# Two transformer blocks on one core: the input issued first on the weights' queue, constants and angles moved into the first down-projection

## The reference, cut to what matters

```python
ang = positions.astype(jnp.float32)[..., None] * inv_freq      # used by the mixer's rope
lower_bounds = jnp.cumsum(jax.nn.softmax(hg_lb_logits, axis=0), axis=0)
h = h + 0.5 * swiglu(rms_norm(h, ln_ffn1[i]), w1_gate[i], w1_up[i], w1_down[i])   # "first SwiGLU"
u = rms_norm(h, ln_mix[i]) @ w_in[i]
...                                                            # hgrn2 + latent attention
h = h + jnp.concatenate([o_hg, o_mla], axis=-1) @ w_out[i]
h = h + 0.5 * swiglu(rms_norm(h, ln_ffn2[i]), w2_gate[i], w2_up[i], w2_down[i])   # "second SwiGLU"
...                                                            # gate, then the second block

def swiglu(x, w_gate, w_up, w_down):
    return (jax.nn.silu(x @ w_gate) * (x @ w_up)) @ w_down
def rms_norm(x, g):
    y = x * lax.rsqrt(jnp.mean(x * x, axis=-1, keepdims=True) + EPS)
    return y * g
```

## Time and profile before

| | us |
|---|---|
| median of 3 runs | 1607.98 (1607.02 to 1611.02) |
| the profiled execution | 1612.58 |
| its span, first to last instruction | 1610.8 |

### The profile page before, as it was taken

One profiled execution on the slowest core, in us unless ns is written; L12 is line 12 of the kernel. 1 busy time (PEld: TensorE's weight loads), 2 busy tenths in 40 slices (PEclk: granted clock), 3 DMA queues, 4 the chain that ended last, 5 costly groups with the idle time before them and its releaser, 6 DMA issues.

```text
span 1610.8 us, 21164 instructions
## 1 busy us (share of the span) xinstructions
PE 1404.9 (87%) x8066; PEld 1074.1 (67%) x8066; DVE 997.7 (62%) x1792; ACT 571.0 (35%) x955; POOL 709.2 (44%) x443
## 2 busy tenths in 40 slices
PE   8799899998999999998999998777777877777776
PEld 8799899978999998888889893333333332333332
DVE  3868434446688544561563577777777777777654
ACT  4554335423444344553443542222222222222212
POOL 2334336421334444386665485444444444444440
PEclk9899899999999999999999999999989999989999
DMA  8677453311576653244323379999999999999994
GB/s 334 216 253 258 159 183 132 131 53 64 180 279 241 248 184 126 68 155 157 104 80 119 107 277 423 421 422 421 422 421 422 421 422 421 422 422 422 421 422 176
DMA packets 59350, 427.15 MB, mean 265 GB/s; under 512 B 6592, under 2 KB 6912, under 8 KB 7936
## 3 DMA queue, kind: packets, MB, share of 16 engines
q0 software_dynamic: 36864, 268.45, 40.2%
q1 hardware_dynamic: 20736, 149.69, 26.4%
q10 hardware_dynamic: 1664, 7.86, 1.2%
HBM read 424.93 MB, written 1.05 MB: 264 GB/s over the span
## 4 chain that ended last, share of the span: by engine, by line
PE 34%; DMA 28%; issue 14%; DVE 13%; POOL 7%; ACT 4%; DVEq 0%; POOLq 0%; SPq 0%; ACTq 0%
DMA rows_x<-in_expert_uv,arena 26%; POOL wlo L326 6%; PE ps L861 4%; PE ps L421 4%; PE ps L864 4%; PE ps L426 4%; PE ps L422 4%; PE ps L498 2%; PE ps L499 2%; PE ps L500 2%; DMA ring<-in_w 2%; DVE arena L1675 1%; ACT whi L937 1%; DVE arena L1347 1%; DVE arena L1491 1%
## 5 line engine op out<-in xcount | busy, mean ns | idle before, releaser
L326 POOL TENSOR_TENSOR wlo<-ring,whi 128x1024 fp32r<-128x1024 f32 x162 | 406.9, 2521 | 512.8 <-ACT whi L937 512.3
L421 PE MATMUL ps<-nh,whi 128*128 128x256 f32 x1440 | 368.1, 292 | 21.6 <-DVE wlo L326 14.1
L937 ACT ACTIVATE whi<-ring 128x1024 fp32r<-128x1024 f32 x236 | 243.5, 1054 | 329.2 <-PE ps L426 130.3
L422 PE MATMUL ps<-nh,wlo 128*128 128x256 f32 x1440 | 358.7, 285 | 0.0
L421 PEld LDWEIGHTS ps<-nh,whi 128*128 128x128 f32 x1440 | 278.3, 193 | 28.6 <-DVE wlo L326 15.1
L422 PEld LDWEIGHTS ps<-nh,wlo 128*128 128x128 f32 x1440 | 278.9, 194 | 0.3
L426 PE MATMUL ps<-nl,whi 128*128 128x256 f32 x1440 | 210.6, 286 | 0.1
L326 DVE TENSOR_TENSOR wlo<-ring,whi 128x1024 fp32r<-128x1024 f32 x74 | 101.3, 1380 | 166.3 <-ACT whi L937 162.3
L426 PEld LDWEIGHTS ps<-nl,whi 128*128 128x128 f32 x1440 | 189.3, 193 | 5.4 <-DVE nl L1288 2.1
L1823 POOL DMA_INDIRECT arena<-in_expert_uv,arena x96 | 112.0, 1166 | 141.2 <-PE ps L864 129.6
L1675 DVE CUSTOM_DVE_ANT_0 arena<-arena 128x1024 f32<-128x1024 f32 x96 | 124.7, 1299 | 39.3 <-DMA arena<-in_expert_uv,arena 35.0
(11 more groups left out here) (324 smaller groups left out, 2426.4 us busy)
## 6 DMA issues: line engine op xcount, KB each, us to landing
ring<-in_w SPq DMA_DIRECT2D x118, 1024.0 KB, 4.9
arena<-in_wmod SPq DMA_DIRECT2D x24, 1024.0 KB, 5.0
small<-in_small ACTq DMA_DIRECT2D x1, 2816.0 KB, 10.8
arena<-in_expert_uv,arena POOLq DMA_INDIRECT x96, 26.8
h<-in_x ACTq DMA_DIRECT2D x1, 1024.0 KB, 7.8
keys<-in_keys ACTq DMA_DIRECT2D x1, 1024.0 KB, 20.8
rows_w<-in_expert_uv,arena POOLq DMA_INDIRECT x64, 25.6
lev_mask<-in_lev_mask ACTq DMA_DIRECT2D x1, 512.0 KB, 11.5
```

What stands on the lines that cost most here:

```text
L326: return v.tensor_tensor(wlo[:, tile % TILES, :], ring[:, tile // 2 % RAW, at:at + TILE], whi[:, tile % TILES, :].bitcast(F32), ALU.subtract)
L421: mm(to, hi[:, k, :], nh[:, k, :], start=(k == 0), stop=False)
L422: mm(to, lo[:, k, :], nh[:, k, :], start=False, stop=False)
L937: fn(whi[:, tile % TILES, :], ring[:, slot % RAW, at:at + TILE], ACT.Copy).then_inc(S("high_w"), 1)
```

## The change

**Input.** SP issues `x` in two halves of four of its eight blocks, ahead of the first two slots of the ring. ACT's squares wait for the half they read. ACT issues only `vec`, `con` and the positions. PE runs 36 matmuls on ones before the squares' sums in place of 26. PE's wait for `con` moves from behind the first SwiGLU to in front of the 12 matmuls on ones.

**Order at the start.** ACT takes the root before it makes the high parts of tiles 0 and 1. DVE takes the reciprocal first, then makes `wlo` of tile 0, then scales.

**Bulk constants.** `load_rest` is gone from ACT. SP issues the same bytes behind seven of the down slots' loads (`load_later`), `small` in three parts.

**Angles and bounds.** They leave the written-out pairs and go behind the residual updates 4, 5 and 6 of the down-projection on DVE; the exponential and the sines go behind squares 4 and 5 on ACT.

```diff
+            def load_later(i):
+
+                if i in (0, 2, 4):
+                    at = slice(i * N_SMALL // 6, (i + 2) * N_SMALL // 6)
+                    sp.dma_start(small[:, at], a["small"][:, at]).then_inc(S("small_landed"), 16)
+                if i == 1:
+                    sp.dma_start(lev_mask[:, :, :], a["lev_mask"]).then_inc(S("small_landed"), 16)
...
+                if i == 6:
+                    sp.dma_start(keys[:, :, :], a["keys"]).then_inc(S("small_landed"), 16)
...
                 for j in range(ahead + 1, slot + 2 * FB + DOWN_SLOTS + RAW):
                     load(j)
-
+                    if mod == 0:
+                        load_later(j - ahead - 4)
+
+            for half in range(2):
+                at = slice(half * C // 2, (half + 1) * C // 2)
+                sp.dma_start(h[:, at, :], a["x"][:, at, :]).then_inc(S(f"x_landed{half}"), 16)
             load(0)
             load(1)
...
             pe.wait_ge(S("constants"), 2)
-            keep_busy(26, bank=5)
+            keep_busy(36, bank=5)
             for c in range(C):
                 square_sum(0, c)
+            pe.wait_ge(S("con_landed"), 16)
             keep_busy(12, bank=5)
 
             swiglu(S_FFN1, 0, 0, 1, 0)
-            pe.wait_ge(S("con_landed"), 16)
...
-            act.dma_start(h[:, :, :], a["x"]).then_inc(S("x_landed"), 16)
...
             for c in range(C):
                 square(0, c)
+            root(0)
             while tile < 2:
                 high(tile)
                 tile += 1
-            root(0)
-
             high_norm(0)
-            load_rest()
...
                 gate(n + 2, 1, before)
-                if before == 0:
-                    bounds_and_sines()
...
             for c in range(C):
                 square(1, c)
+                if c == 4:
+                    bounds_exp()
+                if c == 5:
+                    sines()
...
+            dve.wait_ge(S("vec_landed"), 16)
+            inverse_std(0)
             low(v, dve, 0).then_inc(S("low_dve"), 1)
             tile = 2
-            dve.wait_ge(S("vec_landed"), 16)
-            norm(0, V("ffn1", 0, C), sq, "normed")
+            scaled(0, V("ffn1", 0, C), sq, "normed")
...
-                    if mod == 0:
-                        (angles, bounds)[b]()
...
+                    if mod == 0 and j in (4, 5):
+                        angles(j - 4)
+                    if mod == 0 and j == 6:
+                        bounds()
```

More of the change, by code:

```diff
@@ L880, in _ @@
                           ).then_inc(S("pos_landed"), 16)
[L882 to L891, removed]
             def square(m, c):
                 if m == 0:
-                    act.wait_ge(S("x_landed"), 16)
+                    act.wait_ge(S(f"x_landed{c // (C // 2)}"), 16)
                 else:
@@ L964, in _, with bounds_exp, sines @@
                 tile += 1
-            root(0)
             high_norm(0)
-            load_rest()
-            def bounds_and_sines():
+            def bounds_exp():
                 act.wait_ge(S("lb_shifted"), 1)
                 fn(lb[:, 2:4, :], lb[:, 0:2, :], ACT.Exp).then_inc(S("lb_exp"), 1)
+            def sines():
                 act.wait_ge(S("angle"), 1)
@@ L1258, in inverse_std, with scaled @@
                 own(v.reciprocal(rstd[:, 0, :], std[:, 0, :]))
-            def norm(m, gain, to, sem):
-                inverse_std(m)
+            def scaled(m, gain, to, sem):
                 for c in range(C):
@@ L1264, in norm @@
                                            ALU.mult).then_inc(S(sem), 1)
+            def norm(m, gain, to, sem):
+                inverse_std(m)
+                scaled(m, gain, to, sem)
             tile = 0
@@ L1289, in low_shifted @@
                                            nh[:, c, :].bitcast(F32), ALU.add, ALU.subtract).then_inc(S("low_x"), 1)
+            dve.wait_ge(S("vec_landed"), 16)
+            inverse_std(0)
             low(v, dve, 0).then_inc(S("low_dve"), 1)
             tile = 2
-            dve.wait_ge(S("vec_landed"), 16)
-            norm(0, V("ffn1", 0, C), sq, "normed")
+            scaled(0, V("ffn1", 0, C), sq, "normed")
             low_x(0)
[L1297 to L1308, removed]
-                own(v.tensor_scalar(ang[:, 1, :], ang[:, 2, :], ROUND, None, ALU.subtract))
-                for part in TURN:
-                    own(v.scalar_tensor_tensor(ang[:, 0, :], ang[:, 1, :], -part, ang[:, 0, :], ALU.mult, ALU.add))
-                v.tensor_scalar(ang[:, 0, :], ang[:, 0, :], HALF_TURN, -HALF_TURN, ALU.min, ALU.max
-                                ).then_inc(S("angle"), 1)
@@ new lines, in angles @@
+            def angles(part):
+                if part == 0:
+                    rows = V("lb", 0, 2 * HH).rearrange("p (r h) -> p r h", r=2)
+                    own(v.tensor_tensor(lb[:, 4, :], rows[:, 0, :], rows[:, 1, :], ALU.max))
+                    v.tensor_tensor(lb[:, 0:2, :], rows, over(lb[:, 4, :], 2), ALU.subtract).then_inc(S("lb_shifted"), 1)
+                    dve.wait_ge(S("pos_landed"), 16)
+                    dve.wait_ge(S("con_landed"), 16)
+                    own(v.tensor_copy(ang[:, 1, :], posi[:, :]))
+                    own(v.tensor_scalar(ang[:, 0, :], ang[:, 1, :], K("inv_freq", ROPE), None, ALU.mult))
+                    own(v.tensor_scalar(ang[:, 1, :], ang[:, 0, :], TURN_INV, None, ALU.mult))
+                    own(v.tensor_scalar(ang[:, 2, :], ang[:, 1, :], ROUND, None, ALU.add))
+                else:
+                    own(v.tensor_scalar(ang[:, 1, :], ang[:, 2, :], ROUND, None, ALU.subtract))
+                    for part in TURN:
+                        own(v.scalar_tensor_tensor(ang[:, 0, :], ang[:, 1, :], -part, ang[:, 0, :], ALU.mult, ALU.add))
+                    v.tensor_scalar(ang[:, 0, :], ang[:, 0, :], HALF_TURN, -HALF_TURN, ALU.min, ALU.max
+                                    ).then_inc(S("angle"), 1)
```

11 lines of the change are left out of this document (9 added, 2 removed).

## The result

| | before | after |
|---|---|---|
| median of the timed runs, us | 1611.02 (1607.02 to 1615.54, 7 runs) | 1598.09 (1594.21 to 1602.25, 7 runs) |
| the profiled execution, us | 1612.58 | 1596.27 |
| its span, us | 1610.8 | 1594.5 |

The ratio of after to before is 0.9931, with a 95% interval of 0.9914 to 0.9948: faster by 11 us, or 0.7%. The two profiled executions differ by 16.3. I had forecast 17.6 off the profiled execution, that is 1590.5 by the median, with a range of 1583 to 1601. The direction was right and the time lies in the range, 7.6 us above the forecast.

A forecast was written before the change was run, and what follows sets the result against it. PE was taken to bound the kernel, the first SwiGLU losing 27.1 us against the second. Terms -27.1 + 7.0 + 0.5 + 0.5 + 1.5 = -17.6 gave 1595 profiled, 1590.5 by the median, range 1583 to 1601.

The forecast's parts named there:

- The reading by the twin: First SwiGLU runs the second's code; without bulk constants and angles it should take the second's time, up to -27.1 us.
- My reading of three idle times: PE's waits of 2.78, 8.33 and 3.57 us, with half clock behind them, make 22 to 23 of the 27.1 us.
- the start: From the input to tile 0: more matmuls on ones, low parts and half clock cost +7.0 us together.
- The ten matmuls: Ten more matmuls on ones on PE before the squares' sums end the sums later: +2.4 us, bounds 0 and 3.3.
- The low part of tile 0 and POOL's: At the start, DVE's low part delays the scalings by 1.2 us, POOL's low part of tile 1 by 2.4.
- the rival of a nearly free start: At the start, DVE keeps the ports and extra matmuls are hidden: cost 1.2 to 2.4, time 1585 us; chance 0.14.
- the loop's end at +0.5: First SwiGLU's loop end behaves as the second's, but its modulation-block wait depends on phase: +0.5 us, upper end 5.8.
- the third rival: Only the first 60 us of traffic is cured; the loop's end still waits: gain 5.4, time 1602.5 us; chance 0.12.
- The half clock at tile 0: PE's 4.4 us gap before its first matmul brings half clock there: +1.0 us, bounds 0 and 2.5.
- the ring one slot less ahead: First SwiGLU's start: two tiles ready instead of four, so tiles 2 and 3 may be late: +0.5 us (0 to 3).
- the down slots (+1.5): First SwiGLU's down-projection: moved transfers, table loads and angles are mostly covered: +1.5 us, bounds 0 and 6.
- The slower rival: In the down slots, each extra transfer delays a ring load 2.5 us seven times: +20 us, 1628; chance 0.04.

The follow-up runs named there:

- e1: Kernel after, with SP issuing the ring load of slot 23 before the last modulation block, first SwiGLU only: ratio to the kernel before 0.9892, median 1593.06 us.
- e7: Kernel after, with the start's old order, 14 matmuls on ones before the sums, and slot 23's load ahead of the last modulation block in both SwiGLUs: 0.9829, 1582.74 us.
- e2_bulk_back: Kernel after, with the bulk constants back on ACT's queue behind the eight `nh`, none in the down slots: ratio to the kernel before 0.9976, median 1604.26 us.
- e3_angles_back: Kernel after, with angles, bounds, exponential and sines back in the first SwiGLU's written-out pairs, bulk constants still late: ratio to the kernel before 0.9974, median 1604.62 us.
- e6_loop_loads: Kernel after, plus an unread exponential before the first SwiGLU's loop, which restores two table loads per turn: ratio to the kernel before 0.9936, median 1600.72 us.
- e5: Kernel after, with 26 matmuls on ones before the squares' sums instead of 36, nothing else: ratio to the kernel before 0.9898, median 1593.13 us.
- e4: Kernel after, with the start's order on ACT and DVE as before and 26 matmuls on ones instead of 36: ratio to the kernel before 0.9898, median 1592.59 us.
- e8: e7 with 26 matmuls on ones before the sums instead of 14: ratio to the kernel before 0.9844, median 1585.41 us.
- e10: e7 with 26 instead of 12 matmuls on ones behind the sums: ratio to the kernel before 0.9819, median 1583.09 us.
- e9: e7 with the bulk transfers two down slots earlier, and angles, bounds, exponential and sines one residual update earlier: ratio to the kernel before 0.9805, median 1581.03 us.

## Why the prediction was nearly right

**Confirmed: what bounds the first SwiGLU.** The reading by the twin held. With the edits of e1 the first SwiGLU takes 206.2 us, with those of e7 204.65, where its twins take 205.7 and 204.0. Cut at the same tiles (starts of matmuls on PE: the first of tile 0, of the loop, of the pair behind it, on `gh`, and the last of the squares' sums), the pieces are, in us:

| | up to the loop | loop | last pair | down slots |
|---|---|---|---|---|
| before | 39.5 | 101.8 | 12.0 | 77.9 |
| its twin | 25.5 | 95.8 | 11.5 | 71.2 |
| after | 26.0 | 95.8 | 11.9 | 77.9 |
| e1_exit_order | 26.1 | 95.8 | 12.2 | 70.4 |
| e2_bulk_back | 34.6 | 97.3 | 11.5 | 72.7 |
| e3_angles_back | 31.2 | 97.3 | 12.1 | 74.7 |
| e6_loop_loads | 25.9 | 101.3 | 12.0 | 74.1 |

The wait at the loop's end falls into the last column, which also holds the down slots. Of the 19.5 us that the first SwiGLU gained, 13.4 were in front of the loop and 6.0 in it. Bulk traffic and angles were causes both of the first part (e2, e3). My reading of three idle times left out a fourth, of 2.07 us until 132.44, inside the loop, with a clock of 0.56 and 0.80 in the 5.5 us behind it; the rest of the 6.0 is the half clock that the 8.33 us wait carried into the loop. How much of it the two table loads in each turn made isn't separated: e6 has them and loses 5.5 us in the loop, e3 has them too and its loop takes only 1.5 us longer.

**Confirmed: the start.** The forecast was +7.0, 6.0 of it in front of the first `nh`; measured there are 4.8. The ten matmuls cost 1.6 in this trace and 2.1 in e5, not 2.4: a pass on ones took 10.18 / 72 = 0.14 us, where 26 matmuls had 8.58 / 52 = 0.165. The low part of tile 0 and POOL's were forecast at 3.6 and were 3.2. The scalings took 5.34 us in place of the 3.33 of e4. The rule of the Trainium skill on the shared port (SBUF — State Buffer, SBUF: two separate sides) holds in these rows, but not the reading of it by which DVE's next instruction would keep the port: POOL came in between two instructions of DVE that stood back to back, here and in the sum at 147.94. So the rival of a nearly free start is out.

**The step that failed: the loop's end at +0.5.** It measured about 7.2 us (e1), more than the 5.8 that I had as its upper end. That bound came from two stretches with unlike work, 135 matmuls against 144; cut at the same tiles, the kernel before lost 77.9 - 71.2 = 6.7 us there and 0.5 in the last pair. I took the term from the twin, which has the same order on SP. My text named the risk (its wait depends on phase) and the upper end of 5.8, and the third rival named the wait itself, but dismissed it with the same argument, that the twin has the same blocks.

The order on SP is the cause, and two things set its price. One is whether POOL's low part falls into DVE's sum of a modulation block: where it did, the sum took 5.64 to 5.72 us and PE waited 3.50 to 3.70 (before, after, e3, e6); where it didn't, the sum took 3.61 and PE waited 2.0 to 2.2 (e2, e4, e5). The other is how soon the late load lands: 8.3 to 8.5 us after its issue in the first SwiGLU of before, after and e2 to e6, and 6.9 to 7.1 in the twins of these kernels. Why it lands later isn't shown. The twins waited 0.72 and 0.78 us in the kernels before and after, but 2.2 to 2.3 in e2, e3, e4 and e5, where the twin's sum was the long one (5.63 to 5.72): I had read the twin in a lucky phase.

The idle time of 3.57 at 179.49 in the profile of before had neither bulk constants nor angles near it, which the rival said and I did not follow up. The chain of DVE's sum (162.54), modulation block (168.33) and the ring load behind it could have been read there.

**The third rival's other half was wrong.** It supposed that only the stretch up to the loop is cured, 14.4 us. Its waits there are cured, and the loop's end is not; but the first SwiGLU has gained 19.5 us, 6.0 of them in the loop; the down slots as a whole gained nothing.

**Too dear in this kernel: the small terms.** The half clock at tile 0 (+1.0), the ring one slot less ahead (+0.5) and the down slots (+1.5) were 3.0 together. Over the twin the first SwiGLU has 7.6, of which the loop's end is 7.2; 0.4 are left for the three. For the down slots e7 gives 0.65. By the same measure e8 has 2.8, nearly all of it a wait for the last square, in front of which ACT waited 3.1 us for the ring, and e10 has 2.1, of which that wait is 0.7. In e9, with the transfers two slots earlier, that wait is 0.59 as in the twins. So the +1.5 was not too dear in every phase, and whether the added transfers make the ring late there isn't separated. The slower rival, that each added transfer delays a ring load, needed more than 2 us in each slot; in two slots ACT waited 1.66 and 2.67 us for the ring, and PE had a lead that took all but 0.72. Its price was wrong, too: 17.5 us don't take off the lead of 9 that the text names, which would leave 8.5.

**The sum again.** -27.1 + 4.8 (start) + 7.2 (loop's end) + 0.4 (the rest) = -14.7, the shift of both roots. With the 1.6 us behind the second root it is -16.3, the profiled executions; the timed runs give -11 by the ratio. Against the forecast of -17.6 the traces miss by 1.3: the loop's end 6.7 too cheap, the start 1.2 and the small terms 2.6 too dear, 1.6 not forecast behind the second root. That the miss is so small is luck: the loop's end alone was wrong by 6.7, and 5.4 of other errors stood against it. The median lies 7.6 us above the forecast. Of these, 3.0 are the median of before, 1611.02 in this set and 1607.98 in the one I forecast from; 1.3 are the steps; and 3.4 (the sum gives 1590.4, not 1590.5, hence 7.7) lie between the difference of the profiled executions, 16.3, and that of the medians, 12.9. These last aren't explained. The stretch behind the second root took from 990.4 to 993.8 us in the profiled executions (992.0 before, 990.4 after), whatever the kernel's edits in front of it, so the 1.6 us lie within what it varies by.

## What to carry to other kernels

A twin stage in the same program is a good measure of what a stage should take, but not of a wait that depends on phase, of which one trace is one sample (the twin waited 0.7 us or 2.3 with the same instructions): read the chain behind each long idle time in the slow stage itself, and ask whether the change removes any link of it. A queue that issues in order makes every load wait for what the one in front of it waits for, so a load that is ready goes first. Don't lengthen the work on ones in front of the sums when the input comes earlier; the engine that takes both in order is then what ends last.

## What was not expected of the hardware

GpSimd took its turn in the middle of seven instructions of VectorE, and in front of the first of eight, without a wait between them, and each time stretched them by some 2.0 us, with an instruction of its own of 2.40 in the one case where the row shows its bare length: 5.65 against 3.61, and 5.34 against 3.33. A gap of 3.32 us of PE was followed by half clock (0.50 from 16 to 21 us in e7_combined), and yet to fill it gained nothing; PE then waited 1.5 us for later tiles. And two waits of the same length had unlike prices: behind 3.50 us (the kernel after, 164.77) the clock was low for 11 us of work, behind 3.56 (e6_loop_loads, 170.99) for 3.
